# Out-projection of a two-layer hybrid block: the first two output tiles as a staggered pair, all turned attention outputs through one PSUM buffer

## The chip, the core and the metric

The kernel runs on one core of one Trainium2 chip, as one launch. The metric is the device time of that launch in microseconds (us). Before the change it is 1706.69 us, the median of three runs (1705.18 to 1708.16).

## The reference

The reference is a stack of two layers over 512 latent tokens and 256 context tokens with 1024 features, in float32. Each layer normalises and modulates the tokens, projects them to queries, keys and values of three groups of heads, runs three kinds of attention, and then does what concerns us here:

```
o = concat([window_attention(...), neighbourhood_attention(...), global_block_attention(...)], axis=-1)
x = x + ga_a * (o @ w_out)
x = x + ga_f * swiglu(modulate(rms_norm(x, g_ffn), sh_f, sc_f), w_gate, w_up, w_down)
```

The context tokens get the same treatment in the first layer alone, so the out-projection `o @ w_out` covers 768 tokens in layer 0 and 512 tokens in layer 1. Only the latent stream is returned.

## The kernel before, in words

Every engine has one list of instructions, written out by hand, and the engines meet through semaphores that count upwards (`wait_ge(name, count)`). There is no scheduler: what an engine does next is what the code says next.

Features lie on the 128 partitions for all dense products: an activation is held as 8 feature tiles of 128 partitions by 768 (or 512) tokens. A product is worked off in *units*. A unit is one output tile of 128 features; it sums 8 feature tiles `k = 0..7` in PSUM (`dense`, `dense_tile`). Precision comes from splitting each operand in a high and a low part, so one tile step is three products (high by high, low weight by high, high weight by low), each over one or two ranges of tokens: 6 matmuls in layer 0 (512 and 256 columns), 3 in layer 1 (512 columns). Units alternate between the PSUM buffers `acc[0]` and `acc[1]`, each two banks wide, and between the weight buffers `split_w[0]` and `split_w[1]`. A third buffer of two banks, `side`, serves transposes and small sums.

The out-projection has 8 units per layer. Its activation does not exist yet when it begins. Attention leaves its outputs `o` with tokens on the partitions, so each of the 8 feature tiles has to be turned first:

- TensorE turns tile `m` by 6 (layer 1: 4) transposes into PSUM (`outputs_to_features`, L1194), and counts `ot_ps`.
- ScalarE scales and rounds it to the high part `act[:, 0, m]` (L1544; for tiles 3 and 4, which are stored in column order, L1539 and in layer 0 also L1542), and counts `ot_hi`.
- VectorE computes the rest, `act[:, 1, m]` (L2080; for tiles 3 and 4 L2072 and L2077), and counts `ot_lo`.

Both of them read the same turned tile in PSUM. Before the change the even tiles go to `side` and the odd ones to `acc[1]`, which is free while unit 0 fills `acc[0]`. The transpose of tile `m` may overwrite its buffer when tile `m-2` is through: `pe.wait_ge(ot_lo, l * KT + m - 1)`. Unit 0 runs with `output_tile(k)` ahead of each tile step: it first issues the transposes of tile `k+1`, then waits for tile `k`. Unit 1 needs `acc[1]`, so it waits until all 8 tiles are through, and then runs without a stop.

Around it: at the end of unit 0 TensorE turns a column of bounds (L1219), VectorE takes its maximum (L2091, behind the residual of unit 0, L1784), and at the end of unit 1 TensorE spreads the result (L1222, L1223). GpSimd (POOL) splits the weights of unit `j` (`split`, L723 and L726) once unit `j-2` is done and its raw weights have landed. SP loads the raw weights of unit `j` (`load_out`, L606) once the weights of unit `j-2` are split.

The feed-forward part already has a pair of units that share each tile step (`dense_pair`), and so has the input projection of layer 0, the second unit `LAG = 3` tiles behind.

Of the kernel before, what the change touches and what calls it, by code (L numbers as in the profile page):

```python
# [26 lines left out]
ACT = mybir.ActivationFunctionType  # L27
AX_X = mybir.AxisListType.X

P = 128  # L30
D = 1024
KT = D // P
LAT, CTX = 512, 256
TOK = LAT + CTX
DEPTH = 2
GRID_W, ROWS = 64, 8
# [4 lines left out]
SCALE = HD ** -0.5  # L41
NEG = -1e30
LAG = 3
P_SCALE = 2.0 ** 14
SINK_COL = 127
N_MOD = 6 * KT
# [192 lines left out]
def trunk(nc, x, c, ctx, c_ctx, w_mod, b_mod, norm_attn, norm_ffn, w_in, qk_norm, sink, rpb, w_out,  # L239
# [4 lines left out]
    with ExitStack() as stack:  # L244
        at = [(nc.sbuf_base + 63) // 64 * 64]

        def place(name, shape, dt, where=None):
            size = (2 if dt in (F16, BF16) else 4) * int(np.prod(shape[1:]))
            addr = at[0] if where is None else where
            if where is None:  # L250
                at[0] += (size + 63) // 64 * 64
            return nc.alloc_sbuf_tensor_at(name, shape, dt, offset=addr)

        def sem(name):
            return stack.enter_context(nc.semaphore(name))
# [4 lines left out]
        split_w = [place(f"split_w{i}", [P, 2, 8, P], F32R) for i in range(2)]  # L260
        ident16 = place("ident16", [P, P], BF16)
        ident = place("ident", [P, P], F32)
# [45 lines left out]
        act = place("act", [P, 2, KT, TOK], F32R)  # L308
# [21 lines left out]
        o = place("o", [P, 6, D], F32)  # L330
# [31 lines left out]
        acc = [stack.enter_context(nc.psum_tensor(f"acc{i}", [P, 1024], F32)) for i in range(2)]  # L362
        side = stack.enter_context(nc.psum_tensor("side", [P, 1024], F32))
# [60 lines left out]
        ot_ps, ot_hi, ot_lo = sem("ot_ps"), sem("ot_hi"), sem("ot_lo")  # L424
# [51 lines left out]
        def width(l):  # L476

            return TOK if l < DEPTH - 1 else LAT
# [359 lines left out]
        def _(pe):  # L838
# [112 lines left out]
            def dense_tile(slot, weights, k, n, moving, w, wait_low=None, low=None):  # L951

                for part in (0, 2, 1):
                    if wait_low and part == 1:
                        wait_low(k)
                    for a, b in ((0, 512), (512, TOK))[:1 if w == LAT else 2]:
                        own = low[:, k, :] if low is not None and part == 1 else weights[:, part == 2, k, :]
                        mm = pe.matmul(acc[slot][:, a:b], own,  # L958
                                       moving[:, part == 1, k, a:b],
                                       start=(k == 0 and part == 0), stop=(k == n - 1 and part == 1))  # L960
                if k == n - 1:
                    mm.then_inc(unit_done, 1)

            def dense(slot, weights, n, moving, w, each_k=None, low=None):
                for k in range(n):
                    if each_k:
                        each_k(k)
                    dense_tile(slot, weights, k, n, moving, w, low=low)
# [32 lines left out]
            for l in range(DEPTH):  # L1001
# [69 lines left out]
                for j in range(16):  # L1071
                    if j < 16:
                        u = u_in(l) + j
# [10 lines left out]
                        if j == 0:  # L1084
                            pe.wait_ge(split_ready, ring_of[u] + 2)
                            dense_pair(split_w, act, TOK, in_tile, in_tile_low, 1 if l else LAG)
                        elif j >= 2:
# [100 lines left out]
                def outputs_to_features(m):  # L1188
                    if m == 2:
                        pe.wait_ge(o_ready, outputs_before(l + 1))  # L1190
                    if m >= 2:
                        pe.wait_ge(ot_lo, l * KT + m - 1)
                    for t in range(n_t):
                        mm = pe.transpose((side, acc[1])[m % 2][:, P * t:P * t + P], o[:, t, P * m:P * m + P], ident[:, :])  # L1194
                    mm.then_inc(ot_ps, 1)

                outputs_to_features(0)
# [8 lines left out]
                    if k == KT - 1:  # L1206
                        sum_first_squares(2 * l + 1, width(l))

                for j in range(KT):
                    u = u_out(l) + j  # L1210
                    pe.wait_ge(split_ready, ring_of[u] + 1)
                    if j == 1:
                        pe.wait_ge(ot_lo, (l + 1) * KT)
                    if j >= 2:
                        pe.wait_ge(resid, 32 * l + j - 1)
                    dense(u % 2, split_w[u % 2], 8, act, width(l), output_tile if j == 0 else last_output if j == KT - 1 else None)
                    if j == 0:
                        pe.wait_ge(bound_step, 4 * (l + 1))
                        pe.transpose(mod_ps[0:1, P:2 * P], gain_top[:, 0:1], ident[:, :]).then_inc(bound_turned, 1)  # L1219
                    if j == 1:  # L1220
                        pe.wait_ge(bound_top, l + 1)
                        pe.matmul(mod_ps[:, 2:3], ones[:, :], act_scale[:, l, 0:1], start=True, stop=False)  # L1222
                        pe.matmul(mod_ps[:, 2:3], ones[0:1, :], gain_top[0:1, 1:2], start=False, stop=True).then_inc(bound_ps, 1)  # L1223
                    if j in (3, 4):
                        sum_weights(l, j - 3)
# [5 lines left out]
                for ch, n in enumerate(CHUNKS):  # L1231
# [58 lines left out]
                    for j in range(KT):  # L1290
                        r = n_down(l, ch, j)
# [15 lines left out]
            for t in range(4):  # L1307
# [3 lines left out]
                for k in range(KT):  # L1311
                    mm = pe.transpose(acc[t % 2][:, P * k:P * k + P], x_t[:, k, P * t:P * t + P], ident[:, :])
# [4 lines left out]
        def _(sc):  # L1317
# [6 lines left out]
            for l in range(DEPTH):  # L1324
                r = 64 * l
# [15 lines left out]
            for t in range(LAT // P, TOK // P):  # L1341
                k = 2 + 3 * (t - LAT // P)
# [56 lines left out]
            for l in range(DEPTH):  # L1399
# [53 lines left out]
                for j in range(16):  # L1453
                    take_root(j - 1)
                    swap_halves(j - 3)
                    if j < 16:
                        kind, t, _, _ = QKV[j]
                        slot = (u_in(l) + j) % 2
                        raw = raw_q[j % 3]
                        w = TOK if kind[0] != "q" else width(l)  # L1460
# [3 lines left out]
                        if kind[0] == "v":  # L1464
                            vi = l * 4 + v_before(j)
                            vs = v_scale[:, vi, 0:1]
# [43 lines left out]
                def turned_high(g):  # L1510
# [3 lines left out]
                    for c, (a, b) in enumerate(s["chunks"], upto(g, n_chunks)):  # L1514
                        sc.wait_ge(prob_ps, c + 1)
                        sc.activation(prob_t[g % 4][:, 0, a:b], turned_at[BANK_AT["p", c] % 3][:, 0:b - a], ACT.Copy,  # L1516
                                      scale=P_SCALE).then_inc(prob_hi, 1)

# [15 lines left out]
                w = width(l)  # L1534
                for m in range(KT):
                    vs = v_scale[:, 4 * l + O_V[m], 1:2]
                    sc.wait_ge(ot_ps, l * KT + m + 1)
                    if m in (3, 4):
                        i = sc.activation(act[:, 0, m, 0:LAT].rearrange("p (r c) -> p c r", r=ROWS),  # L1539
                                          (side, acc[1])[m % 2][:, 0:LAT].rearrange("p (c r) -> p c r", r=ROWS), ACT.Copy, scale=vs)  # L1540
                        if w == TOK:
                            i = sc.activation(act[:, 0, m, LAT:TOK], (side, acc[1])[m % 2][:, LAT:TOK], ACT.Copy, scale=vs)  # L1542
                    else:
                        i = sc.activation(act[:, 0, m, 0:w], (side, acc[1])[m % 2][:, 0:w], ACT.Copy, scale=vs)  # L1544
                    i.then_inc(ot_hi, 1)

                sc.activation(root_first[:, :], eps[:, 0:1], ACT.Sqrt)
# [109 lines left out]
        def _(ve):  # L1657
# [132 lines left out]
            for l in range(DEPTH):  # L1790
                w = width(l)
# [68 lines left out]
                def largest(j):  # L1860
# [11 lines left out]
                    ve.reciprocal(v_scale[:, i, 0:1], v_scale[:, i, 1:2])  # L1872
                    ve.tensor_scalar(v_scale[:, i, 1:2], v_scale[:, i, 1:2], 1.0 / P_SCALE, None, ALU.mult).then_inc(v_scaled, 1)

# [57 lines left out]
                def turned_low(g):  # L1932
                    s = STEPS[g]
                    for c, (a, b) in enumerate(s["chunks"], upto(g, n_chunks)):
                        ve.wait_ge(prob_hi, c + 1)
                        ve.scalar_tensor_tensor(out=prob_t[g % 4][:, 1, a:b], in0=turned_at[BANK_AT["p", c] % 3][:, 0:b - a],  # L1936
                                                scalar=P_SCALE, in1=prob_t[g % 4][:, 0, a:b], op0=ALU.mult, op1=ALU.subtract
                                                ).then_inc(prob_lo, 1)
# [129 lines left out]
                for m in range(KT):  # L2068
                    vs = v_scale[:, 4 * l + O_V[m], 1:2]
                    ve.wait_ge(ot_hi, l * KT + m + 1)  # L2070
                    if m in (3, 4):
                        i = ve.scalar_tensor_tensor(out=act[:, 1, m, 0:LAT].rearrange("p (r c) -> p c r", r=ROWS),  # L2072
                                                    in0=(side, acc[1])[m % 2][:, 0:LAT].rearrange("p (c r) -> p c r", r=ROWS), scalar=vs,
                                                    in1=act[:, 0, m, 0:LAT].rearrange("p (r c) -> p c r", r=ROWS).bitcast(F32),
                                                    op0=ALU.mult, op1=ALU.subtract)
                        if w == TOK:
                            i = ve.scalar_tensor_tensor(out=act[:, 1, m, LAT:TOK], in0=(side, acc[1])[m % 2][:, LAT:TOK], scalar=vs,  # L2077
                                                        in1=act[:, 0, m, LAT:TOK].bitcast(F32), op0=ALU.mult, op1=ALU.subtract)
                    else:
                        i = ve.scalar_tensor_tensor(out=act[:, 1, m, 0:w], in0=(side, acc[1])[m % 2][:, 0:w], scalar=vs,  # L2080
                                                    in1=act[:, 0, m, 0:w].bitcast(F32), op0=ALU.mult, op1=ALU.subtract)
                    i.then_inc(ot_lo, 1)

# [158 lines left out]
```

## Time and profile before

| | |
|---|---|
| median of three runs | 1706.69 us |
| the profiled execution | 1705.99 us |
| its span, first to last instruction | 1704.2 us |
| TensorE busy | 1632.2 us, 96% |
| VectorE busy | 1025.6 us, 60% |
| ScalarE busy | 745.2 us, 44% |
| GpSimd busy | 739.6 us, 43% |
| mean granted TensorE clock | 0.985 |

The profiled execution lies 0.70 us under the median. The out-projection of layer 0 begins at about 387 us of the span and that of layer 1 at about 1284 us. The matmul spans of the profile are modelled at their ends, so 96% busy does not mean that TensorE runs at its peak.

In the rows below PE is TensorE, PEld its weight loads, DVE is VectorE, ACT is ScalarE, POOL is GpSimd. `acc` and `side` are the PSUM buffers, with buffer numbers left out: `acc<-ident,o` is a transpose into `acc[1]`, `acc<-act,split_w` a matmul of a unit.

### The profile page before, as it was taken

How to read it: one execution, taken by the hardware profiler on the slowest of the kernel's cores; microseconds unless marked ns; L12 is line 12 of the kernel's file. 1: busy time of each engine (PE TensorE's matmuls, PEld its weight loads, DVE VectorE, ACT ScalarE, POOL GpSimd, SP SyncE). 2: the span in 40 equal slices, each digit the busy share in tenths (PEclk: the TensorE clock that was granted, in tenths of full speed). 3: DMA queues.
4: the chain of work that ended last, by engine and by line, in shares of the span. 5: the costliest groups of instructions: out<-in, count | busy, mean ns of one | idle time of the engine just before them, and what ended most of it. 6: DMA issues, size and time to landing. Idle time of an engine off the chain costs nothing.

```text
span 1704.2 us, 29725 instructions
## 1 busy us (share of the span) xinstructions
PE 1632.2 (96%) x11685; PEld 1120.3 (66%) x11685; DVE 1025.6 (60%) x2075; ACT 745.2 (44%) x1367; POOL 739.6 (43%) x474
## 2 busy tenths in 40 slices
PE   7999989998999999999999999997998899999998
PEld 3688878977856656666666667886887544444444
DVE  3434498884479873788358855456995526326234
ACT  4222278884144341334313323225894455355342
POOL 1244335572614443344433343550403567567563
PEclk9999999999989999999999999998999899999999
DMA  9355453323045412353326232554103242243222
GB/s 325 58 133 138 118 150 98 94 63 88 26 123 161 137 56 93 99 164 120 113 75 225 79 69 53 135 135 114 28 6 101 62 136 87 75 136 96 66 87 87
DMA packets 317290, 179.24 MB, mean 105 GB/s; under 512 B 88527, under 2 KB 310495, under 8 KB 317151
## 3 DMA queue, kind: packets, MB, share of 16 engines
q1 hardware_dynamic: 284542, 143.63, 30.6%
q10 hardware_dynamic: 32608, 33.71, 6.2%
q8 instruction: 93, 1.52, 0.4%
q14 instruction: 47, 0.38, 0.1%
HBM read 158.97 MB, written 2.83 MB: 95 GB/s over the span
## 4 chain that ended last, share of the span: by engine, by line
PE 73%; DVE 15%; issue 5%; ACT 3%; DMA 2%; SPq 1%; POOL 1%; ACTq 0%; DVEq 0%; POOLq 0%
PE acc L958 60%; DVE mod_acc L2148 4%; DVE prob L1930 2%; DVE prob_t L1936 2%; PE small L905 2%; PE mod_ps L1058 1%; PE side L1143 1%; PE side L895 1%; ACT prob_t L1516 1%; PE acc L1126 1%; PE acc L1127 1%; DVE mod_acc L2146 1%; ACT prob L1494 1%; DMA tokens<-in_ctx 1%; PE mod_ps L1143 1%
## 5 line engine op out<-in xcount | busy, mean ns | idle before, releaser
L958 PE MATMUL acc<-act,pair_w 128*128 128x512 f16 x3168 | 580.2, 345 | 5.6 <-ACT act L1395 3.5
L958 PEld LDWEIGHTS acc<-act,pair_w 128*128 128x128 f16 x3168 | 309.5, 99 | 265.5 <-issue 10.6
L958 PE MATMUL acc<-act,split_w 128*128 128x512 f32 (+1 forms) x1920 | 378.6, 355 | 9.3 <-DVE act L2080 4.6
L958 PEld LDWEIGHTS acc<-act,split_w 128*128 128x128 f32 x1920 | 307.7, 189 | 63.6 <-DVE act L2080 6.8
L799 POOL TENSOR_SCALAR pair_raw<-pair_raw,weight_scale 128x1024 f32<-128x1024 f32 x88 | 109.6, 1246 | 324.9 <-ACT pair_w L1566 324.9
L958 PE MATMUL acc<-hidden,down_w 128*128 128x512 f16 (+1 forms) x1056 | 247.8, 343 | 1.6 <-DVE hidden L2114 0.8
L723 POOL TENSOR_SCALAR split_w<-raw_w 128x1024 fp32r<-128x1024 f32 x72 | 77.1, 1071 | 342.9 <-PE acc L958 231.0
L2148 DVE SCALAR_TENSOR_TENSOR mod_acc<-mod_chunk,silu_c,mod_acc 128x256 f32<-128x256 f32 x280 | 198.0, 751 | 4.0
L802 POOL TENSOR_TENSOR pair_w<-pair_raw,pair_w 128x1024 f16<-128x1024 f32 x88 | 192.4, 2187 | 7.3
L726 POOL TENSOR_TENSOR split_w<-raw_w,split_w 128x1024 fp32r<-128x1024 f32 x72 | 171.9, 2388 | 6.0
L2109 DVE SCALAR_TENSOR_TENSOR prod<-acc,prod_scale,silu_g 128x768 f32<-128x768 f32 (+1 forms) x44 | 38.9, 884 | 208.0 <-PE acc L958 199.0
L958 PEld LDWEIGHTS acc<-hidden,down_w 128*128 128x128 f16 x1056 | 100.5, 98 | 85.2 <-POOL down_w L818 2.8
L958 PE MATMUL acc<-hidden,down_low 128*128 128x512 f16 (+1 forms) x528 | 152.6, 343 | 0.0
L1635 ACT ACTIVATE hidden<-prod 128x768 f16<-128x768 f32 (+1 forms) x44 | 32.4, 736 | 238.4 <-DVE prod L2109 238.4
L1494 ACT ACTIVATE prob<-prob,stat 128x768 f32<-128x768 f32 (+5 forms) x160 | 121.7, 761 | 32.7 <-DVE prob L1930 25.8
L1930 DVE TENSOR_SCALAR_CACHE_REDUCE prob<-acc,score_scale 128x768 f32<-128x768 f32 (+4 forms) x128 | 102.7, 802 | 12.0 <-PE acc L1127 9.2
L1566 ACT ACTIVATE pair_w<-pair_raw,weight_scale 128x1024 f16<-128x1024 f32 x88 | 95.9, 1137 | 16.5 <-DVE weight_scale L2027 16.5
L1555 ACT ACTIVATE squares_out<-pair_raw 128x1024 bf16<-128x1024 f32 x88 | 92.4, 1050 | 7.5 <-DMA pair_raw<-in_w_up 3.5
L1784 DVE SCALAR_TENSOR_TENSOR x_t<-acc,down_gate,x_t 128x512 f32<-128x512 f32 x72 | 45.4, 658 | 80.4 <-PE acc L958 80.2
L1628 ACT ACTIVATE silu_g<-acc,weight_scale 128x768 f32<-128x768 f32 (+1 forms) x44 | 34.6, 786 | 132.9 <-PE acc L958 99.5
L1126 PE MATMUL acc<-ks,qs 128*128 128x256 f16 (+1 forms) x384 | 91.6, 270 | 0.0
L1127 PE MATMUL acc<-ks,qs 128*128 128x256 f16 (+1 forms) x384 | 89.3, 269 | 0.0
(229 smaller groups left out, 2462.8 us busy)
## 6 DMA issues: line engine op xcount, KB each, us to landing
mod_chunk<-in_w_mod ACTq DMA_DIRECT2D x28, 1024.0 KB, 5.2
pair_raw<-in_w_gate SPq DMA_DIRECT2D x44, 512.0 KB, 3.7
pair_raw<-in_w_up SPq DMA_DIRECT2D x44, 512.0 KB, 4.8
raw_w<-in_w_in SPq DMA_DIRECT2D x64, 256.0 KB, 3.8
raw_w<-in_w_mod SPq DMA_DIRECT2D x24, 512.0 KB, 4.0
raw_w<-in_w_down SPq DMA_DIRECT2D x20, 512.0 KB, 4.5
mod_start<-in_w_mod SPq DMA_DIRECT2D x8, 1024.0 KB, 11.0
ks<-q_split SPq DMA_DIRECT2D x64, 96.0 KB, 2.4
```

The source lines that it names most:

```text
L723: pool.tensor_scalar(split_w[slot][:, 0, 0:n, :], raw_w[slot][:, 0:n, :], 1.0, 0.0, ALU.mult, ALU.add).then_inc(hi_w, 1)
L726: pool.tensor_tensor(split_w[slot][:, 1, 0:n, :], raw_w[slot][:, 0:n, :], split_w[slot][:, 0, 0:n, :].bitcast(F32), ALU.subtract).then_inc ...
L799: pool.tensor_scalar(raw, raw, weight_scale[:, 1, 2 * f + s:2 * f + s + 1], 0.0, ALU.mult, ALU.add).then_inc(weight_mul, 1)
L802: pool.tensor_tensor(w[:, s, 1, :, :], raw, w[:, s, 0, :, :], ALU.subtract).then_inc(pair_ready, 1)
L958: mm = pe.matmul(acc[slot][:, a:b], own, moving[:, part == 1, k, a:b], start=(k == 0 and part == 0), stop=(k == n - 1 and part == 1))
L1126: pe.matmul(out_, q, ks[:, s["k"], 0, k0:k0 + size], start=True, stop=False)
L1127: mm = pe.matmul(out_, q, ks[:, s["k"], 1, k0:k0 + size], start=False, stop=not masks)
L1494: sc.activation(p, p, ACT.Exp, bias=stat[:, 1, i:i + 1], scale=-1.0, accum_out=stat[:, 2, i:i + 1]).then_inc(exps, 1)
L1555: sc.activation(squares_out[:, :], pair_raw[home(f)][:, s, :, :].rearrange("p k n -> p (k n)"), ACT.Square, accum_out=weight_sum[:, 2 * f ...
L1566: sc.activation(pair_w[home(f)][:, s, 0, :, :], pair_raw[home(f)][:, s, :, :], ACT.Copy, scale=weight_scale[:, 1, 2 * f + s:2 * f + s + 1] ...
L1930: ve.tensor_scalar(out_, src, minus, None, ALU.mult, ALU.min, accum_out=lowest).then_inc(scored, 1)
L2148: s = ve.scalar_tensor_tensor(**kw, in1=kw["out"], op0=ALU.mult, op1=ALU.add)
```

## The change

Three things change, all in the out-projection and in both layers.

1. All 8 turned tiles go through `side`. The transposes of tile `m` (from `m = 1` on) wait until tile `m-1` is through ScalarE and VectorE, where before those of tile `m` (from `m = 2` on) waited for tile `m-2`.
2. Units 0 and 1 are issued together: tile step `k` of unit 0, and behind it, from `k = 3` on, tile step `k-3` of unit 1. After the last step of unit 0 four steps of unit 1 are left.
3. What stood between the two units, the transpose of the bounds, now stands behind both, directly ahead of the two small matmuls that need its result.

```
+LAG_OUT = LAG
...
 def outputs_to_features(m):
     if m == 2:
         pe.wait_ge(o_ready, outputs_before(l + 1))
-    if m >= 2:
-        pe.wait_ge(ot_lo, l * KT + m - 1)
+    if m >= 1:
+        pe.wait_ge(ot_lo, l * KT + m)
     for t in range(n_t):
-        mm = pe.transpose((side, acc[1])[m % 2][:, P * t:P * t + P], o[:, t, P * m:P * m + P], ident[:, :])
+        mm = pe.transpose(side[:, P * t:P * t + P], o[:, t, P * m:P * m + P], ident[:, :])
     mm.then_inc(ot_ps, 1)
...
-for j in range(KT):
+for j in range(1, KT):
     u = u_out(l) + j
     pe.wait_ge(split_ready, ring_of[u] + 1)
     if j == 1:
-        pe.wait_ge(ot_lo, (l + 1) * KT)
-    if j >= 2:
+        w0, w1 = split_w[(u - 1) % 2], split_w[u % 2]
+        for k in range(KT + LAG_OUT):
+            if k < KT:
+                output_tile(k)
+                dense_tile((u - 1) % 2, w0, k, KT, act, width(l))
+            if k >= LAG_OUT:
+                dense_tile(u % 2, w1, k - LAG_OUT, KT, act, width(l))
+    else:
         pe.wait_ge(resid, 32 * l + j - 1)
-    dense(u % 2, split_w[u % 2], 8, act, width(l), output_tile if j == 0 else last_output if j == KT - 1 else None)
-    if j == 0:
+        dense(u % 2, split_w[u % 2], 8, act, width(l), last_output if j == KT - 1 else None)
+    if j == 1:
         pe.wait_ge(bound_step, 4 * (l + 1))
         pe.transpose(mod_ps[0:1, P:2 * P], gain_top[:, 0:1], ident[:, :]).then_inc(bound_turned, 1)
...
-i = sc.activation(act[:, 0, m, 0:w], (side, acc[1])[m % 2][:, 0:w], ACT.Copy, scale=vs)
+i = sc.activation(act[:, 0, m, 0:w], side[:, 0:w], ACT.Copy, scale=vs)
...
-            in0=(side, acc[1])[m % 2][:, 0:w], scalar=vs,
+            in0=side[:, 0:w], scalar=vs,
```

The other lines of the diff make the same replacement of `(side, acc[1])[m % 2]` by `side` for tiles 3 and 4. No instruction is added to or taken from any engine's work; they move, and their waits change.

TensorE's list in layer 0, from the first transposes on. `split_w_52` holds the weights of unit 0, `split_w_53` those of unit 1. Before:

```order
L1194 MATMUL side<-ident,o 128x128 [waits exps,o_ready]
L1194 MATMUL side<-ident,o 128x128 x5
L1194 MATMUL acc<-ident,o 128x128 [waits split_ready]
L1194 MATMUL acc<-ident,o 128x128 x5
L958 MATMUL acc<-act,split_w_52 128x512 [waits ot_lo]
...
L1194 MATMUL side<-ident,o 128x128 [waits ot_lo,o_ready]
L1194 MATMUL side<-ident,o 128x128 x5
```

and with the change (its lines are one higher):

```order
L1195 MATMUL side<-ident,o 128x128 [waits exps,o_ready]
L1195 MATMUL side<-ident,o 128x128 x5
L1195 MATMUL side<-ident,o 128x128 [waits ot_lo,split_ready]
L1195 MATMUL side<-ident,o 128x128 x5
L959 MATMUL acc<-act,split_w_52 128x512 [waits ot_lo]
...
L1195 MATMUL side<-ident,o 128x128 [waits ot_lo,o_ready]
L1195 MATMUL side<-ident,o 128x128 x5
```

The transposes stand in the same places. Those of tile 1 now wait for `ot_lo` of tile 0 and write to `side`, like all the later ones.

TensorE's list around the fourth tile step (`k = 3`) of unit 0, before:

```order
L1194 MATMUL side<-ident,o 128x128 [waits ot_lo]
L1194 MATMUL side<-ident,o 128x128 x5
L958 MATMUL acc<-act,split_w_52 128x512 [waits ot_lo]
L958 MATMUL acc<-act,split_w_52 128x256
...
L1194 MATMUL acc<-ident,o 128x128 [waits ot_lo]
L1194 MATMUL acc<-ident,o 128x128 x5
```

and with the change:

```order
L1195 MATMUL side<-ident,o 128x128 [waits ot_lo]
L1195 MATMUL side<-ident,o 128x128 x5
L959 MATMUL acc<-act,split_w_52 128x512 [waits ot_lo]
L959 MATMUL acc<-act,split_w_52 128x256
...
L959 MATMUL acc<-act,split_w_53 128x512
L959 MATMUL acc<-act,split_w_53 128x256
...
L1195 MATMUL side<-ident,o 128x128 [waits ot_lo]
L1195 MATMUL side<-ident,o 128x128 x5
```

A tile step of unit 1 (6 matmuls with `split_w_53`) now stands between the step of unit 0 and the next transposes.

TensorE's list at the end of units 0 and 1. Before, the transpose of the bounds stands between the units, 48 matmuls ahead of its users:

```order
L1219 MATMUL mod_ps<-ident,gain_top 1x128 [waits bound_step]
L958 MATMUL acc<-act,split_w_53 128x512 [waits ot_lo,split_ready]
L958 MATMUL acc<-act,split_w_53 128x256
...
L1222 MATMUL mod_ps<-act_scale,ones 128x1 [waits bound_top]
L1223 MATMUL mod_ps<-gain_top,ones 128x1
L958 MATMUL acc<-act,split_w_52 128x512 [waits resid,split_ready]
```

and with the change it stands directly ahead of them:

```order
L959 MATMUL acc<-act,split_w_53 128x512
L959 MATMUL acc<-act,split_w_53 128x256
L1226 MATMUL mod_ps<-ident,gain_top 1x128 [waits bound_step]
L1229 MATMUL mod_ps<-act_scale,ones 128x1 [waits bound_top]
L1230 MATMUL mod_ps<-gain_top,ones 128x1
L959 MATMUL acc<-act,split_w_52 128x512 [waits resid,split_ready]
```

## Rows read from the trace of the kernel before

**Rows 1.** The page's chain that ended last, shares of the span by line.

```profile
PE acc L958 60%; DVE mod_acc L2148 4%; DVE prob L1930 2%; DVE prob_t L1936 2%; PE small L905 2%; PE mod_ps L1058 1%; PE side L1143 1%; PE side L895 1%; ACT prob_t L1516 1%; PE acc L1126 1%; PE acc L1127 1%; DVE mod_acc L2146 1%; ACT prob L1494 1%; DMA tokens<-in_ctx 1%; PE mod_ps L1143 1%
```

**Rows 2.** Chain of waits, layer 0: start us, us on the chain, what.

```profile
387.05 0.70 PE side L1194 x6
...
387.78 0.91 ACT act L1544
...
388.71 1.03 DVE act L2080
...
389.78 1.32 PE acc L958 x6
391.10 0.67 PE side L1194 x6
...
391.80 0.91 ACT act L1544
...
395.80 1.14 ACT act L1539
...
397.21 1.12 DVE act L2072
...
398.77 1.32 PE acc L958 x6
...
405.94 8.43 PE acc L958 x48
```

**Rows 3.** Timeline, layer 0: start us, us, engine, line, operation.

```profile
384.40 0.66 PE L1143 MATMUL side<-ident,prob 128*128 128x128 f32 x4 [0.45 <-ACT prob L1494]
...
385.15 0.60 ACT L1516 ACTIVATE prob_t<-side 128x512 f16<-128x512 f32 x1 [0.32 <-PE side L1143]
...
386.89 0.85 PE L1194 MATMUL side<-ident,o 128*128 128x128 f32 x6
...
390.82 0.70 PEld L1194 LDWEIGHTS side<-ident,o 128*128 128x128 f32 x6
...
406.93 0.27 DVE L2091 TENSOR_REDUCE gain_top<-mod_ps 1x1 f32<-1x128 f32 x1
```

**Rows 4.** Timeline, layer 1, the first tile.

```profile
1283.82 0.64 PE L1194 MATMUL side<-ident,o 128*128 128x128 f32 x4
...
1284.49 0.69 ACT L1544 ACTIVATE act<-side,v_scale 128x512 fp32r<-128x512 f32 x1 [1.81 <-PE side L1194]
...
1285.21 0.75 DVE L2080 SCALAR_TENSOR_TENSOR act<-side,v_scale,act 128x512 fp32r<-128x512 f32 x1
```

**Rows 5.** Chain of waits, layer 1.

```profile
1286.02 0.96 PE acc L958 x3
...
1290.43 1.17 ACT act L1539
1291.62 1.10 DVE act L2072
...
1292.77 0.97 PE acc L958 x3
...
1297.93 5.59 PE acc L958 x24
```

**Rows 6.** Timeline, layer 1: splitting and loading weights.

```profile
1297.99 1.05 POOL L723 TENSOR_SCALAR split_w<-raw_w 128x1024 fp32r<-128x1024 f32 x1 [64.33 <-PE acc L958]
...
1301.55 9.58 SPq L606 DMA_DIRECT2D raw_w<-in_w_out  x12
```

**Rows 7.** The instructions of line L606: from issue to landing.

```profile
DMA to landing us min/median/max: 2.3/2.6/4.7
```

**Rows 8.** Stretches: length, busy PE, PEld, DVE, ACT, POOL, PE clock, DMA share, GB/s.

```profile
386.90:391.00 4.10, 2.71 (x25) 2.35 (x21) 3.22 (x8) 1.69 (x2) 0.00 (x0) 1.00 0.50 142
...
467.00:470.00 3.00, 1.44 (x13) 1.34 (x12) 1.14 (x2) 0.94 (x2) 0.36 (x1) 1.00 0.49 143
470.00:474.00 4.00, 3.10 (x14) 2.71 (x13) 1.17 (x3) 0.27 (x1) 0.00 (x0) 0.52 1.15 343
```

More of the change, by code:

```diff
@@ L1539, in _ @@
                         i = sc.activation(act[:, 0, m, 0:LAT].rearrange("p (r c) -> p c r", r=ROWS),
-                                          (side, acc[1])[m % 2][:, 0:LAT].rearrange("p (c r) -> p c r", r=ROWS), ACT.Copy, scale=vs)
+                                          side[:, 0:LAT].rearrange("p (c r) -> p c r", r=ROWS), ACT.Copy, scale=vs)
                         if w == TOK:
-                            i = sc.activation(act[:, 0, m, LAT:TOK], (side, acc[1])[m % 2][:, LAT:TOK], ACT.Copy, scale=vs)
+                            i = sc.activation(act[:, 0, m, LAT:TOK], side[:, LAT:TOK], ACT.Copy, scale=vs)
                     else:
-                        i = sc.activation(act[:, 0, m, 0:w], (side, acc[1])[m % 2][:, 0:w], ACT.Copy, scale=vs)
+                        i = sc.activation(act[:, 0, m, 0:w], side[:, 0:w], ACT.Copy, scale=vs)
                     i.then_inc(ot_hi, 1)
@@ L2072, in _ @@
                         i = ve.scalar_tensor_tensor(out=act[:, 1, m, 0:LAT].rearrange("p (r c) -> p c r", r=ROWS),
-                                                    in0=(side, acc[1])[m % 2][:, 0:LAT].rearrange("p (c r) -> p c r", r=ROWS), scalar=vs,
+                                                    in0=side[:, 0:LAT].rearrange("p (c r) -> p c r", r=ROWS), scalar=vs,
                                                     in1=act[:, 0, m, 0:LAT].rearrange("p (r c) -> p c r", r=ROWS).bitcast(F32),
@@ L2076, in _ @@
                         if w == TOK:
-                            i = ve.scalar_tensor_tensor(out=act[:, 1, m, LAT:TOK], in0=(side, acc[1])[m % 2][:, LAT:TOK], scalar=vs,
+                            i = ve.scalar_tensor_tensor(out=act[:, 1, m, LAT:TOK], in0=side[:, LAT:TOK], scalar=vs,
                                                         in1=act[:, 0, m, LAT:TOK].bitcast(F32), op0=ALU.mult, op1=ALU.subtract)
                     else:
-                        i = ve.scalar_tensor_tensor(out=act[:, 1, m, 0:w], in0=(side, acc[1])[m % 2][:, 0:w], scalar=vs,
+                        i = ve.scalar_tensor_tensor(out=act[:, 1, m, 0:w], in0=side[:, 0:w], scalar=vs,
                                                     in1=act[:, 0, m, 0:w].bitcast(F32), op0=ALU.mult, op1=ALU.subtract)
```

## The prediction

> **What bounds the kernel now.** I read the chain that ended last first. Matmuls of the dense units are 60% of it [rows 1], so in most places time is saved only where TensorE works less or waits less. Then I read the chain of waits over the out-projection. In layer 0 it does not stay on TensorE while unit 0 runs: it goes from transposes to ScalarE's rounding, to VectorE's subtraction and back to a tile step, again and again [rows 2]; in layer 1 the same [rows 5]. As soon as unit 1 begins, at 405.94, the chain is matmuls without a gap: 8.43 us for its 48 matmuls in layer 0, 5.59 us for 24 in layer 1 [rows 2, 5]. So what counts is how long a turned tile takes on its way round, how many rounds stand one behind the other, and what TensorE does meanwhile.
>
> The stages of one round, taken from start to start so that the hand-overs are in them:
>
> - Transposes to ScalarE, layer 0: from 386.89 to 387.78, 0.89 us [rows 2, 3]; layer 1: from 1283.82 to 1284.49, 0.67 us [rows 4].
> - ScalarE to VectorE: 387.78 to 388.71, 0.93 us [rows 2]; layer 1: 1284.49 to 1285.21, 0.72 us [rows 4].
> - VectorE to TensorE: 388.71 to 389.78, 1.07 us [rows 2]; layer 1: 1285.21 to 1286.02, 0.81 us [rows 4, 5].
> - Tiles 3 and 4, which are reordered: 395.80 to 397.21 and on to 398.77, 1.41 and 1.56 us [rows 2]; layer 1: 1290.43 to 1291.62 to 1292.77, 1.19 and 1.15 us [rows 5].
>
> A full round is then 0.89 + 0.93 + 1.07 = 2.89 us in layer 0 and 2.20 us in layer 1; for tiles 3 and 4 it is 3.86 and 3.01 us.
>
> **One buffer in place of two.** Before, the transposes of tile 1 ran right behind those of tile 0, and each later tile was turned while the one before was still being read. With the change the transposes of tile m wait for VectorE to finish tile m-1, so 8 rounds stand in a row. Tile 0 keeps its time: TensorE is free for the next step at 389.78 in layer 0 and at 1286.02 in layer 1 [rows 2, 5]. Then follow 7 rounds, 5 common and 2 long:
>
> - layer 0: 5 x 2.89 + 2 x 3.86 = 22.17 us; the last step of unit 0 begins at 389.78 + 22.17 = 411.95;
> - layer 1: 5 x 2.20 + 2 x 3.01 = 17.02 us; it begins at 1286.02 + 17.02 = 1303.04.
>
> **The pair.** A tile step costs TensorE 8.43 / 8 = 1.05 us in layer 0 and 5.59 / 8 = 0.70 us in layer 1 [rows 2, 5]. From k = 3 on, TensorE has one set of transposes (0.70 us of weight loads [rows 3]) and two steps per round: 0.70 + 2 x 1.05 = 2.80 us, just under the round of 2.89 us, so in layer 0 the rounds set the pace and TensorE almost keeps it busy. In layer 1 it is at most 0.67 + 1.40 = 2.07 us against 2.20 us. So four steps of unit 1 are hidden inside the rounds. After the last wait come one step of unit 0, which takes 1.32 us when it starts on an idle engine (0.96 us in layer 1) [rows 2, 5], and the last four of unit 1:
>
> - layer 0: 411.95 + 1.32 + 4 x 1.05 = 417.5. Before, unit 1 ended at 405.94 + 8.43 = 414.37. That is 3.1 us later.
> - layer 1: 1303.04 + 0.96 + 4 x 0.70 = 1306.8. Before: 1297.93 + 5.59 = 1303.52. That is 3.3 us later.
>
> What the pair hides, four steps of unit 1 (4.2 and 2.8 us), is less than what the rounds lose by no longer overlapping: the last step of unit 0 begins 411.95 - 404.5 = 7.4 us later in layer 0 (404.5 is 405.94 less the step of 1.32 us and the short transpose between).
>
> **The bounds.** Before, the maximum over the turned bounds lay beside unit 1 and cost nothing. Now TensorE has nothing between its transpose and the two matmuls that need the maximum; behind those stands all of unit 2. On the way are VectorE's 0.27 us [rows 3], two hand-overs of 0.04 us, and the start on an idle engine, which made a step 1.32 in place of 1.05 us: 0.27 + 0.08 + 0.27 = 0.6 us per layer. From below it is the first two, 0.35 us; from above I allow 0.9 us, a full transposes-to-reader stage more in place of the start. VectorE itself is free: it is through with the residual of unit 0 about 2 us before the pair ends.
>
> **What is queued behind.** GpSimd may split unit 2's weights when unit 0 is done, in layer 1 at 1303.04 + 0.96 = 1304.0. Before, it took from 1297.99 to 1301.55, when SP was released by it: 3.56 us [rows 6]. So it ends at 1307.7, and TensorE wants it at 1306.8 + 0.5 (the three small matmuls) + 0.6 = 1307.9. SP may load unit 4 from 1307.7: half of 9.58 us of issues [rows 6] and 2.6 us to landing [rows 7] give 1315.1, the split 1318.7; TensorE wants it two units later, at 1307.9 + 11.3 = 1319.2. Both fit with a few tenths to spare, cost nothing in my sum, and have their price among the rivals. In layer 0 the units are 8.43 us long and there are microseconds to spare. All that follows (residuals, sums of squares, the feed-forward weights) is released by the ends of units and shifts with them; I see no wait there that would swallow the delay, since the chain is on TensorE through units 1 to 7.
>
> **The sum**: 3.1 + 3.3 + 2 x 0.6 = 7.6 us. The profiled execution took 1705.99 us and would take 1713.6; it lay 0.7 us under the median, so on the median the forecast is 1706.69 + 7.6 = 1714.3 us.
>
> **The price of transposes after a wait** is the term that the trace does not show for this place: in the old order nearly all of them followed other work. From above: four transposes of another line, issued after a wait, took from 384.40 to 385.15 until ScalarE began, 0.75 us [rows 3], where I take 0.67; 14 rounds x 0.08 = 1.1 us more, 1715.4. From below: transposes that followed a step needed 391.10 to 391.80, 0.70 us [rows 2], where I take 0.89. That saves 0.19 us in each of 7 rounds of layer 1, in 4 rounds of layer 0, and in the other 3 only 0.09 us, since TensorE itself needs 2.80: 2.3 us less, 1712.0. I take 0.89, since the first transposes, in row 386.89, are the only ones of this shape that begin a round.
>
> The Trainium skill, page "TensorE: Matmul & The Clock Gate", section "Part 2: What happens when you issue a matmul", says that the queue pulls weight loads ahead of matmuls still in flight. If that held for transposes behind a semaphore, the lower figure would be right and the sum 5.3 us. The trace speaks against it: row 389.78, after a wait, has the step at 1.32 us, against 1.05 us inside a stream.
>
> **Rivals.**
>
> *TensorE's clock falls in the pair.* For it: from 467 to 470 TensorE was busy 1.44 of 3.00 us, and in the next 4 us the granted clock was 0.52, so near the lower level of 1.2 GHz [rows 8]. With the change the first 2.9 us of layer 0 hold only 0.89 us of transposes, and 386.9 to 391 about 2.1 busy us in place of 2.71. Against it: that stretch had the full clock, 1.00 [rows 8], and attention before it keeps TensorE busy. Price: transposes and step tails stretch by some 0.6 us a round for two or three rounds in each layer, 3 us in all: 1717.3 us. The skill's same page, "Part 1: The HAM clock gate", has the throttled state as the default and activity as what releases it; by that rule this change, which spreads idle time over the pair, risks more than one that gathers it. No row here has this mixture of work.
>
> *The weights of units 2 or 4 come late in layer 1.* The margins above are 0.2 and 0.5 us. With the slowest landing seen, 4.7 us [rows 7], unit 4 would be 1.6 us late: 1715.9 us.
>
> *The rounds do not lengthen, and the idle time is filled.* This is the case on the other side. If ScalarE and VectorE took a tile as fast as before and only the pair mattered, unit 0 would end as before and five steps of unit 1 would be inside it: -5.3 us in layer 0 and -3.5 us in layer 1, with the bounds -7.6 us, so 1699.1 us. It decides where the seven rounds of layer 0 fall under 414.37 - 0.6 - 1.32 - 4.2 - 389.78 = 18.5 us, 2.6 us each where I have 3.2 on average. Against it: ScalarE and VectorE alone are 0.93 + 1.07 = 2.00 us of a common round and 2.97 us of a long one, one after the other on the same tile, and that leaves a common round 0.4 us for its transposes, less than any row shows.
>
> *TensorE sets the pace and transposes are cheap*: the lower case above, 1712.0 us.
>
> **How the numbers follow.** Forecast and its own bounds (1712.0 to 1715.4, with the bounds' cost at 0.35 instead of 0.6 down to 1711.5): 0.62, of which 0.15 for the cheap transposes. Clock 0.14. Late weights 0.09. Filled idle time 0.04. The rest, 0.11, is something smaller that I have not seen, such as a stall before that the delay swallows; half of it still slower. The range for 8 in 10 is 1710.8 to 1717.8. No change that a measurement of this kernel can tell is 0.2%, 3.4 us: 1703.3 to 1710.1. Slower 0.90, same 0.06, faster 0.04.
>
> **What would show it.** In the profile after: transposes of each tile start within 0.1 us of VectorE's end of the tile before; starts of ScalarE's L1544 rows 2.9 us apart in layer 0 and 2.2 us in layer 1; the last step of unit 0 near 412 and the end of unit 1 near 417.5; VectorE's maximum between two neighbouring small operations of TensorE, with TensorE idle over half a microsecond. I am wrong if the rounds are under 2.6 us, if the clock falls between 387 and 418, or if the span after 480 differs in length from before, which would put the cause elsewhere.

## The result, and the profile after

The changed kernel takes 1715.74 us, the median of 5 runs (1711.46 to 1716.17), against 1706.69 us for 5 runs of the kernel before: a ratio of 1.0048, 95% interval 1.0036 to 1.0061. Measured again later (`changed_again` below) the ratio was 1.0069 (1.0055 to 1.0082). It is slower, by some 8 to 12 us. The forecast was 1714.3 us in a range of 1710.8 to 1717.8, with 0.90 on slower.

The profiled execution has a span of 1713.9 us. The distances below are read from the timelines; T0 and T7 are the starts of the transposes of tiles 0 and 7, and unit 2 is the start of its first matmul.

| us | before | after | forecast |
|---|---|---|---|
| layer 0, T0 to T7 | 14.76 | 24.23 | 22.2 |
| layer 0, T0 to unit 2 | 27.83 | 33.78 | 31.7 |
| layer 1, T0 to T7 | 10.89 | 18.51 | 17.0 |
| layer 1, T0 to unit 2 | 20.06 | 25.59 | 24.1 |

The difference of the two spans, 9.7 us, is 5.95 us in layer 0 and 5.53 us in layer 1, less 1.8 us elsewhere: 1.27 us more ahead of T0 in layer 0, 2.46 us less between the two out-projections, 0.6 us less behind the second.

The chain of waits through the pair of layer 0 in the profile after (start us, us, what) shows the rounds in a row:

```profile
388.32 0.70 PE side L1195 x6
...
389.05 0.91 ACT act L1551
...
389.98 1.03 DVE act L2087
...
391.14 0.86 PE side L1195 x6
...
392.03 0.91 ACT act L1551
392.94 0.02 issue
392.96 1.03 DVE act L2087
...
394.13 1.53 PE side L1195 x6
...
397.69 1.56 PE side L1195 x6
...
402.22 1.10 PE side L1195 x6
403.32 3.45 PE acc L959 x12
...
412.45 0.81 PE side L1195 x6
413.27 7.57 PE acc L959 x42
420.83 0.12 PE mod_ps L1226
420.96 0.02 issue
420.98 0.29 DVE gain_top L2098
...
421.31 0.38 PE mod_ps L1229 x2
421.70 0.31 PE mod_ps L1230 x2
422.01 17.02 PE acc L959 x96
```

Against [rows 2] the reader sees three things. Every round but one now begins with transposes that wait for VectorE: 0.04 to 0.14 us after its row ends, six transposes start. (The exception is tile 5, at 406.77, behind twelve matmuls that the lower clock drew out to 3.45 us. For tiles 6 and 7 the chain runs through TensorE alone, because its rows are modelled at their ends; the first weight load of these transposes too begins 0.05 us after VectorE's row.) The stages of ScalarE and VectorE are the same to 0.01 us (0.91 and 1.03). And the transposes, 0.86 us at 391.14, take 1.53 and 1.56 us in the next two rounds. At the end the maximum of VectorE, 0.29 us, stands alone on the path, as it did not at 406.93 in [rows 3].

The stretches of both pairs, with the same columns as [rows 8]:

```profile
388.10:391.10 3.00, 0.91 (x14) 0.67 (x10) 2.30 (x7) 0.90 (x1) 0.00 (x0) 1.00 0.23 60
391.10:394.10 3.00, 2.25 (x12) 1.69 (x13) 1.02 (x1) 0.90 (x1) 0.00 (x0) 0.73 1.15 345
394.10:397.70 3.60, 3.45 (x13) 2.78 (x13) 1.02 (x1) 0.90 (x1) 0.00 (x0) 0.50 0.95 230
397.70:402.20 4.50, 2.67 (x12) 2.27 (x12) 1.46 (x2) 1.40 (x2) 0.00 (x0) 0.82 0.43 130
402.20:406.50 4.30, 4.28 (x18) 3.75 (x19) 1.50 (x2) 1.39 (x2) 0.00 (x0) 0.60 0.00 0
...
1290.90:1293.60 2.70, 2.33 (x7) 1.53 (x8) 0.75 (x1) 0.69 (x1) 0.00 (x0) 0.50 1.12 336
```

The granted clock fell to 0.50, its lower level of 1.2 GHz, in both layers. In the profile before it was 1.00 over both stages. So two of the cases of the prediction hold at once: the rounds, and the clock.

### The profile page after: what moved, and what is told of

Read it like the earlier page. It is cut to its first block, busy times and chain, and to the rows that moved or that the text cites. A ratio compares the mean times of both kernels' runs of the same rounds, so it can differ in the third digit from the quotient of the medians.

```text
span 1713.9 us, 29725 instructions
## 1 busy us (share of the span) xinstructions
PE 1638.3 (96%) x11685; PEld 1122.6 (65%) x11685; DVE 1023.7 (60%) x2075; ACT 744.9 (43%) x1367; POOL 740.2 (43%) x474
## 4 chain that ended last, share of the span: by engine, by line
PE 73%; DVE 15%; issue 5%; ACT 4%; DMA 2%; SPq 1%; POOL 1%; DVEq 0%; ACTq 0%; POOLq 0%
PE acc L959 60%; DVE mod_acc L2155 4%; DVE prob L1937 2%; DVE prob_t L1943 2%; PE small L906 2%; PE mod_ps L1059 1%; PE side L1144 1%; PE side L896 1%; ACT prob_t L1523 1%; PE acc L1127 1%; PE acc L1128 1%; DVE act L1764 1%; PE side L1195 1%; DVE scaled_ffn L1780 1%; DVE mod_acc L2153 1%
## 5 line engine op out<-in xcount | busy, mean ns | idle before, releaser
L1127 PE MATMUL acc<-ks,qs 128*128 128x256 f16 (+1 forms) x384 | 91.1, 269 | 0.0
L1943 DVE SCALAR_TENSOR_TENSOR prob_t<-side,prob_t 128x512 f16<-128x512 f32 (+2 forms) x152 | 84.1, 564 | 8.0 <-ACT prob_t L1523 5.4
```

The source lines that it names most:

```text
L1127: pe.matmul(out_, q, ks[:, s["k"], 0, k0:k0 + size], start=True, stop=False)
```

## The experiments

Each was timed against the kernel before on its own chip. One_buffer, lag1, filler and bounds_early ran on one chip, changed_again, before_again, lag1_short_split and both two_buffers kernels on another; so versions of the two groups are compared by their ratios and stages, not by their times. The last two columns are the mean granted clock over the two stages; in the kernel before it was 1.00 in both, in two profiles.

| kernel | ratio (95%) | layer 0: T7, unit 2 | layer 1: T7, unit 2 | clock 0 | clock 1 |
|---|---|---|---|---|---|
| changed | 1.0048 (1.0036-1.0061) | 24.23, 33.78 | 18.51, 25.59 | 0.84 | 0.86 |
| changed_again | 1.0069 (1.0055-1.0082) | 22.46, 31.99 | 18.64, 25.72 | 1.00 | 0.87 |
| one_buffer | 1.0108 (1.0093-1.0123) | 24.61, 37.71 | 18.47, 27.71 | 0.82 | 0.88 |
| lag1 | 1.0069 (1.0054-1.0084) | 23.05, 31.00 | 17.75, 24.63 | 0.95 | 0.93 |
| filler | 1.0061 (1.0047-1.0074) | 22.40, 31.93 | 17.23, 24.32 | 1.00 | 1.00 |
| bounds_early | 1.0069 (1.0056-1.0082) | 22.47, 31.38 | 18.02, 24.94 | 1.00 | 0.93 |
| lag1_short_split | 1.0040 (1.0027-1.0053) | 22.49, 30.43 | 18.99, 24.68 | 1.00 | 0.86 |
| two_buffers | 0.9994 (0.9985-1.0003) | 17.26, 26.12 | 12.31, 19.18 | 1.00 | 1.00 |
| two_buffers_lags | 0.9989 (0.9980-0.9998) | 17.97, 25.90 | 11.57, 19.34 | 1.00 | 1.00 |
| before_again | 1.0002 (0.9992-1.0013) | 14.77, 27.83 | 10.86, 20.03 | 1.00 | 1.00 |

Each row of distances is one execution. The same stage repeats well at the full clock (27.83 twice; 31.93 and 31.99). The rest of the program does not: between unit 2 of layer 0 and T0 of layer 1 these ten profiles and the first one need 866.6 to 871.8 us, without a change there. A total is therefore good to 1 or 2 us, and the theories are told apart by the stages.

### One buffer, no pair

```
-mm = pe.transpose((side, acc[1])[m % 2][:, P * t:P * t + P], ...)
+mm = pe.transpose(side[:, P * t:P * t + P], ...)
-if m >= 2:
-    pe.wait_ge(ot_lo, l * KT + m - 1)
+if m >= 1:
+    pe.wait_ge(ot_lo, l * KT + m)
```

> The kernel before with all turned tiles through side, and nothing else: units 0 and 1 one after the other. Theory (rounds): the eight rounds stand in a row, so the last step of unit 0 begins 7.4 us later in layer 0 and 6.2 us later in layer 1, and nothing hides it: at least 1706.7 + 13.6 = 1720.3 us, and up to 4 us more if TensorE's clock falls in the gaps as it did in the changed kernel's profile. Rival (the pair is what costs, one buffer is harmless): within 1 us of the kernel before.

1722.86 us against 1704.37 us for the kernel before: 18.5 us more, 0.9 us above the upper end of what was expected with a falling clock. T0 to unit 2 grew by 9.9 and 7.7 us; 2.2 us of the 9.9 us are the clock, since T0 to T7 is 24.61 us here and 22.40 us with the same rounds at the full clock (filler, below). The single buffer alone is the loss, and the pair gives part of it back, net of what the bounds cost there: 3.9 us in layer 0 (37.71 to 33.78) and 2.1 us in layer 1. The rival falls.

### Filling TensorE's gaps

```
+def fill(count):
+    for i in range(count):
+        pe.matmul(acc[1][:, 0:512], w0[:, 0, i % 8, :],
+                  w0[:, 0, 0:4, :].rearrange("p a b -> p (a b)"), start=True, stop=True)
+fill(8 if l == 0 else 6)
...
     dense_tile((u - 1) % 2, w0, k, KT, act, width(l))
+    if k < 3:
+        fill(3)
```

> The changed kernel with extra matmuls of 512 columns, whose results are overwritten, in TensorE's gaps: 8 (layer 1: 6) behind the first transposes, 3 behind each of the first three steps of unit 0. They add work that fits in the gaps (8 x 0.22 us in 2.1 us, 3 x 0.22 us in 0.95 us). Theory (the clock fell for want of work, and cost about 2.1 us in layer 0 and 1.5 us in layer 1): granted clock 1.00 through both pairs, the pairs 30.6 and 23.0 us long from the first transposes to the end of unit 1 where the profile showed 32.7 and 24.5 us, and 1715.7 - 3.6 = 1712.1 us. Rival (the longer stages have another cause): the same length of pair or more, 1715.7 us or slower.

The stages of filler, at the full clock:

```profile
388.10:418.80 30.70, 27.64 (x166) 22.43 (x162) 11.48 (x18) 12.54 (x16) 3.47 (x2) 1.00 0.31 86
1288.10:1311.20 23.10, 19.97 (x102) 14.31 (x98) 8.48 (x14) 9.75 (x14) 2.44 (x2) 1.00 0.42 114
```

and the same of the changed kernel:

```profile
388.10:420.80 32.70, 27.86 (x153) 23.22 (x149) 11.49 (x18) 12.55 (x17) 3.47 (x2) 0.84 0.29 81
1288.60:1313.10 24.50, 19.04 (x86) 13.34 (x82) 8.48 (x14) 9.83 (x14) 2.58 (x2) 0.86 0.39 107
```

With 17 extra matmuls in layer 0 and 15 in layer 1 the stages are 1.85 and 1.27 us shorter, T0 to unit 2, and the transposes after a wait take what the prediction gave them (start us, us, timeline of TensorE):

```profile
390.95 0.87 PE L1195 MATMUL side<-ident,o 128*128 128x128 f32 x6 [0.21 <-DVE act L2096]
```

So 3.1 us of the 11.5 us that the two stages lost in the profile of the changed kernel are the clock. The total does not show it: 1714.37 us is 10.0 us over the kernel before on that chip, where 1712.1 us, 5.4 us over the first runs of the kernel before, had been expected. What was saved in the stages is smaller than the scatter of the rest; that the whole program gains from the filling is not shown.

### The same kernels again

> The changed kernel itself once more, on the chip of the runs that it is to be compared with, and a second profile of it. If the time that filler and lag1 lost or won is real, this lies about 3 us above filler; expected 8 to 12 us above the kernel before. The granted clock in the two pairs may fall in other stretches than in the first profile: where it holds at 1.00 the distance from the first transposes to unit 2 should be 31.9 us in layer 0 and 24.3 us in layer 1, as in filler.

> The kernel before itself once more, for a second profile. Theory: its two out-projections hold the full clock, with 27.8 us and 20.1 us from the first transposes to unit 2, and the first transposes of layer 0 begin within 1 us of 388.1 us, as in all profiles since, where the first profile had 386.9 us; then that 1.2 us is no effect of the change. Rival: 386.9 us again, and the change or its surroundings move something in the attention ahead of it.

changed_again kept the full clock in layer 0 and lost it in layer 1. Its layer 0 is the clean case of the changed code, and its chain has the long rounds of tiles 3 and 4:

```profile
395.00 0.89 PE side L1195 x6
...
395.91 1.16 ACT act L1546
...
397.35 1.08 DVE act L2079
...
398.87 0.89 PE side L1195 x6
```

395.00 to 398.87 is 3.87 us; the prediction had 3.86. T0 to unit 2 is 31.99 us (expected 31.9). Its total is 11.1 us over the kernel before, within the expected 8 to 12. In before_again T0 of layer 0 is at 388.08, not 386.9: the 1.27 us ahead of the change is no effect of it. changed_again, with T0 at 386.14, says the same from the other side.

### The bounds turned earlier

```
+if k == KT - 1:
+    pe.wait_ge(bound_step, 4 * (l + 1))
+    pe.transpose(mod_ps[0:1, P:2 * P], gain_top[:, 0:1], ident[:, :]).then_inc(bound_turned, 1)
```

> The changed kernel with the transpose of the bounds directly behind the last step of unit 0, four steps of unit 1 ahead of its users. Theory: VectorE's maximum is hidden again, 0.6 us less per layer, 1715.7 - 1.3 = 1714.4 us, and in the profile the matmuls of unit 2 follow within 0.5 us of the last of unit 1. Rival (the three small operations cost what they cost wherever they stand): no difference in that stretch, 1715.7 us.

As expected for the stage, layer 0 takes 8.91 us from T7 to unit 2, against 9.53 in filler and changed_again: 0.6 us saved, as the prediction priced it. The chain has no VectorE between the units:

```profile
414.97 4.21 PE acc L959 x24
419.19 0.12 PE mod_ps L1229 x2
419.30 0.31 PE mod_ps L1230 x2
419.61 3.58 PE acc L959 x19
```

Layer 1 takes 6.92 us, against 7.08 and 7.09: only 0.2 us. The timeline of TensorE names what came in its place:

```profile
1310.48 0.38 PE L1230 MATMUL mod_ps<-gain_top,ones 1*128 1x1 f32 x2
1311.28 1.90 PE L959 MATMUL acc<-act,split_w 128*128 128x512 f32 x7 [0.42 <-POOL split_w L727]
```

Unit 2 waited for its weights. The total is a miss: 1716.82 us, 12.4 us over the kernel before on its chip, where 7.7 us over the first runs of the kernel before had been expected. A total cannot show 0.8 us, and this one does not show it.

### Unit 1 one tile behind, and the weights of unit 2

```
-LAG_OUT = LAG
+LAG_OUT = 1
```

> The changed kernel with unit 1 one tile behind unit 0 in place of three. Two fewer steps of unit 1 stand behind the last round: -2 x 1.05 us in layer 0, -2 x 0.70 us in layer 1, so 1715.7 - 3.5 = 1712.2 us by the rounds alone. If the clock fell because the early rounds were thin, steps in rounds 1 and 2 keep it up more of the time: 1709 to 1711 us, and the profile shows transposes of 0.9 us rather than 1.5 us after a wait. Rival (TensorE sets the pace, not the rounds): the same work in the same time, no change from 1715.7 us.

Layer 0: 1.6 us from T7 to unit 2 saved of the 2.1 expected (7.95 against 9.53). The other 0.5 us is a wait for weights too, which the prediction had not seen for this layer (start us, us, timeline of TensorE):

```profile
419.25 3.99 PE L959 MATMUL acc<-act,split_w 128*128 128x512 f32 x21 [0.46 <-POOL split_w L727]
```

In layer 1 it is 6.88 us against 7.09: of 1.4 us all but 0.2 is gone. The waits of TensorE between 1288 and 1315 us (us in total, times, longest):

```profile
PE side L1195 <- DVE act L2087: 2.4, 4, 1.7
...
PE acc L959 <- POOL split_w L727: 1.1, 1, 1.1
```

The total is 1715.10 us, 10.7 us over the kernel before on its chip, where 5.5 us by the rounds alone, and less with a better clock, had been expected: a miss.

To test that GpSimd alone is what stands there, this kernel leaves out seven eighths of the splitting of that one unit's weights. It computes something else, and serves for the stage alone:

```
 for j in range(1 + l, KT):
-    split(u_out(l) + j, 8)
+    split(u_out(l) + j, 1 if l == 1 and j == 2 else 8)
```

> The kernel with unit 1 one tile behind, where in layer 1 GpSimd splits only one of the eight feature tiles of unit 2's weights (the other seven stay as they were). Theory (in layer 1 unit 2 waited for GpSimd, and that swallowed what the shorter lag should have saved): from the last transposes to unit 2 it takes 3.2 + 1.4 + 1.1 = 5.7 us in place of 6.9 us, and TensorE's idle time before unit 2 has no POOL in it. Rival (the wait for the bounds alone): 6.9 us as before.

5.69 us from T7 to unit 2, where 5.7 was expected, and no wait for POOL:

```profile
1312.67 0.38 PE L1229 MATMUL mod_ps<-act_scale,ones 128*128 128x1 f32 x2 [0.37 <-DVE gain_top L2098]
1312.98 0.38 PE L1230 MATMUL mod_ps<-gain_top,ones 1*128 1x1 f32 x2
1313.29 0.97 PE L959 MATMUL acc<-act,split_w 128*128 128x512 f32 x3
```

The clock in lag1 was higher on average than in the changed kernel (0.95 and 0.93), but in its variant 0.86 in layer 1 with the same order of TensorE's work. One tile step earlier does not keep the clock up reliably.

### The pair with two buffers

The odd tiles go to the two banks of `small` and `mod_ps`, placed side by side, and the bounds are turned behind unit 0:

```
+rest = stack.enter_context(nc.psum_tensor("rest", [P, 1024], F32))
+small, mod_ps = rest[:, 0:512], rest[:, 512:1024]
...
-if m == 2:
+if m == 1:
     pe.wait_ge(o_ready, outputs_before(l + 1))
-if m >= 1:
-    pe.wait_ge(ot_lo, l * KT + m)
+if m >= 2:
+    pe.wait_ge(ot_lo, l * KT + m - 1)
 for t in range(n_t):
-    mm = pe.transpose(side[:, P * t:P * t + P], ...)
+    mm = pe.transpose((side, rest)[m % 2][:, P * t:P * t + P], ...)
```

> The pair with two buffers for the turned tiles: odd tiles go to the two banks that small and mod_ps occupy, so tile m waits for tile m-2 as in the kernel before, and the transpose of the bounds stands behind unit 0's last step. Theory (one buffer was the whole loss, and the idle time of unit 0 can be filled): TensorE sets the pace from the fourth tile on, 2.80 us a tile in layer 0, so 26.5 us from the first transposes to unit 2 in place of 27.8; in layer 1 the weights of unit 2, split 3.7 us after unit 0 ends, allow 17.4 us in place of 20.1. In all 4 us less than the kernel before, and the clock stays up. Rival (TensorE has its hands full and gains nothing from the pair): equal to the kernel before within 1 us.

The chain of layer 0 from the fifth tile on is TensorE alone:

```profile
398.26 0.65 PE rest L1195 x6
398.92 2.09 PE acc L959 x12
401.00 0.65 PE side L1195 x6
401.66 2.09 PE acc L959 x12
403.74 0.66 PE rest L1195 x6
404.40 3.37 PE acc L959 x18
```

0.65 + 2.09 = 2.74 us a tile, and the stage is 26.12 us (expected 26.5). The same pair with one buffer needed 31.38 us (bounds_early, also at the full clock): the second buffer is worth 5.3 us there. In layer 1 it is 19.18 us where 17.4 us had been expected: unit 2 waits for POOL again, at 6.87 us behind T7, the same as in lag1. I had put the end of unit 0 1.7 us too early, because I counted TensorE's work without its waits in the first rounds. Of the 4 us expected the stages give 2.6, the total about 1 (ratio 0.9994), which the interval does not tell from no change.

```
-LAG_OUT = LAG
+LAG_OUT = (2, 5)
...
-if k >= LAG_OUT:
+if k >= LAG_OUT[l]:
```

> The kernel with two buffers for the turned tiles, with unit 1 two tiles behind unit 0 in layer 0 and five behind in layer 1 (it was three in both). In layer 0 TensorE still had gaps of 0.3 and 0.7 us before the third and fourth step, which one more step of unit 1 can fill: 25.5 us from the first transposes to unit 2 in place of 26.1. In layer 1 unit 2 waited for its weights, which are split once unit 0 is done; with a lag of five unit 0 is done earlier and more of unit 1 stands behind it: 18.1 us in place of 19.2. Together 1.7 us less than two_buffers, 3.7 us less than the kernel before in the two stages, a ratio near 0.998. Rival (what is saved there is lost in the place of unit 1's steps): 26.1 and 19.2 us again.

25.90 and 19.34 us, where 25.5 and 18.1 us had been expected: 0.2 us less than two_buffers in layer 0, nothing in layer 1. That is the rival's 26.1 and 19.2 us rather than the theory's. The wait for POOL is gone there, but now six steps of unit 1 stand behind the last step of unit 0 (18 matmuls, 4.43 us), and TensorE's gaps of 0.4 to 0.5 us ahead of the early steps are left unfilled. The lag only moves work from one side of the last round to the other. Its median is 1704.33 us against 1705.76 us, ratio 0.9989 (0.9980 to 0.9998): of all versions the only one whose interval lies below 1, by 0.0002. Its median equals that of two_buffers (1704.33 us), so a gain from the lags is not shown.

## Why the prediction was right

**One buffer in place of two: right.** At the full clock the last transposes stand 22.40 us (filler) and 22.46 us (changed_again) behind the first in layer 0, forecast 22.2; 17.23 us in layer 1 (filler), forecast 17.0. Most of the difference is at tiles 1 and 2, whose transposes wait for two semaphores: their two rounds took 2.99 us each in changed_again where 2.89 was taken. one_buffer shows that this is the cause of the loss and not the pair.

**Transposes after a wait: the value taken was right, in part by luck.** 0.86 to 0.89 us in filler and changed_again, and 0.88 to 0.91 us with the hand-over to ScalarE, as the prediction counted its 0.89. But row 386.89 of [rows 3], from which it was taken, has no idle time ahead of it: it stood behind other matmuls and showed this value all the same. The lower bound is refuted for this place: the six transposes took 0.89 us behind a wait and 0.65 us behind other work (two_buffers). So is the reading by which the rule of the Trainium skill, page "TensorE: Matmul & The Clock Gate", section "Part 2: What happens when you issue a matmul", on weight loads that are pulled ahead would reach over a semaphore.

**The pair: right.** From T7 to unit 2 in layer 0 9.53 us (filler, changed_again), forecast 9.5; in layer 1 7.09 us (filler), forecast 7.1.

**The bounds: right in layer 0** (0.6 us, bounds_early). In layer 1 the same 0.6 us could not be had back, since the weights of unit 2 come 0.2 us behind. The prediction had that margin as 0.2 us, and it is what lag1, bounds_early and two_buffers ran into. In layer 0 it saw microseconds to spare; there were 1.6 us (changed_again), and lag1 used them up. In the changed kernel itself the weights were in time.

**The clock: a rival with 0.14, and it happened.** It was priced at 3 us and cost 3.1 us in the profile (1.85 and 1.27 us, against filler). The failure is in the chance, and in treating it as a rival of the forecast instead of an addition to it. The row that should have weighed more is the stretch 467 to 470 of [rows 8]: TensorE busy for 1.44 of 3.00 us, and a clock of 0.52 right behind it. The prediction held against it that attention before had kept TensorE busy, and in no single-buffer profile was that enough in both layers: of the six without filling (changed, changed_again, one_buffer, lag1, bounds_early, lag1_short_split) three kept 1.00 in layer 0 and none in layer 1. The Trainium skill, page "TensorE: Matmul & The Clock Gate", section "HAM oscillation — how this bites in real kernels", warns of idle gaps of TensorE; here the longest gap in the pair was 2.14 us (ahead of 391.14), and the clock fell all the same. Filling the gaps with any matmuls kept it, in one profile. That idle time which is spread risks more than idle time which is gathered, as the prediction put it, is not shown: no run compares the two.

**What was not forecast**: the sum of the remaining stages differs by 1.8 us between the two profiles, with no instruction changed in them. before_again and changed_again show such differences between executions of one kernel, both ahead of the change and behind it. Much of it goes with the clock: between the two out-projections the eleven profiles have 17 to 34 us at the lower level, in code that did not change, and the longer that is, the longer the stage (correlation 0.81, about 0.27 us for each us). The first profile of the changed kernel has the least of all, 17.1 us, against 30.7 us in the first one before. Whether a clock loss in the pair makes one later less likely stays open; no run tests it. At the full clock the two stages of the change cost 4.1 and 4.3 us, 8.4 us against 7.6 us forecast (31.96 - 27.83, and 24.32 - 20.06; 31.96 is the mean of filler and changed_again).

**What was luck.** Two of the three signs by which the prediction wanted to be called wrong came true in the profile: the clock fell between 387 and 418 us, and the rest of the span had another length. The total came near the forecast because these offset each other: 8.4 us in the stages at the full clock, 3.1 us for the clock, less 1.8 us elsewhere. The upper end of the range is 11.1 us over the kernel before. In the later measurements changed_again lies 11.1 us over it, filler 10.0 us and bounds_early 12.4 us, so that on those chips the forecast of 7.6 us is low. What is well borne out are the stages; the total is borne out less well.

## What to carry to other kernels

When a buffer that three engines hand round is cut from two copies to one, count rounds, not busy time: each tile pays the sum of all its stages, and work put beside it only refunds what it fits in. Before filling idle time, look at what the moved end releases: here the next unit's weights, split by GpSimd 3.7 us after the first unit's end, had 0.2 us of slack in layer 1 and swallowed there nearly all that was saved behind the last round. And when a change spreads TensorE's work thin, add the clock's fall to the forecast rather than setting it against it.

## What the runs showed of the hardware

- TensorE's granted clock fell to 0.50, its level of 1.2 GHz, with TensorE's rows busy for 2.25 of 3.00 us (391.1 to 394.1), after a stretch with 0.91 of 3.00 us. After a second fall it came back, for the rest of the stage, between 402.2 and 406.5, with TensorE busy for 4.28 of 4.30 us. The longest gap was 2.14 us.
- Six fp32 transposes of 128 x 128 take 0.86 to 0.89 us behind a semaphore, 0.65 us behind other matmuls (two_buffers), and 1.53 to 1.56 us behind a semaphore at the lower clock.
- A hand-over from VectorE to TensorE costs more when TensorE's instruction waits for two semaphores. From VectorE's last row to the first transpose it was 0.15 us for tiles 1 and 2, which wait for two, and 0.05 to 0.06 us for tiles 3 to 7, which wait for one; on the chain these are 0.14 and 0.04 us. So it is in both layers of all seven single-buffer profiles, at either clock, wherever TensorE was not itself the later. In filler, where the second wait of tile 1 has moved to an extra matmul ahead of it, tile 1 too has 0.05 us.
